# Expert queries in three goes instead of two, with tile 1's scores and tile 0's exponential between the second and the third

## The reference

```python
def peer_ffn(h, lp):
    q = (x @ lp['peer_wq']).reshape(t, PEER_HEADS, 2, PEER_HALF)          # 8 heads, 2 x 64
    sc = jnp.einsum('thpd,hpnd->thpn', q, lp['peer_subkeys'])             # 128 keys each
    sv, si = lax.top_k(sc, PEER_TOPK)                                     # 16
    cand = (sv[:, :, 0, :, None] + sv[:, :, 1, None, :]).reshape(t, PEER_HEADS, 256)
    top_v, top_p = lax.top_k(cand, PEER_TOPK)
    experts = jnp.take_along_axis(cidx, top_p, axis=-1)
    gates = jax.nn.softmax(top_v, axis=-1)
    # per token: sum over its 128 experts of gate * gelu(x . u[e]) * v[e]
```

## Time and profile before

| | us |
|---|---|
| median of 3 runs | 4885.16 |
| lowest and highest | 4881.96, 4885.67 |
| the profiled execution | 4879.89 |
| its span on the core | 4877.8 |

### The profile page before, as it was taken

How to read it: one execution, slowest core, us unless ns; L and a number is a source line. 1 busy time by engine, 2 the same in 40 slices (tenths; PEclk the granted TensorE clock), 3 DMA queues, 4 the chain that set the end, 5 groups by cost and what they waited for, 6 DMA issues and landing times.

```text
span 4877.8 us, 65715 instructions
## 1 busy us (share of the span) xinstructions
PE 4086.6 (84%) x23446; PEld 3534.7 (72%) x23446; DVE 3535.7 (72%) x6335; ACT 1394.0 (29%) x1987; POOL 1808.1 (37%) x1075
## 2 busy tenths in 40 slices
PE   6889999724499999999878999996336999999996
PEld 5866888423389888998767678883225898889885
DVE  2417224699989999999942272256998999999998
ACT  3236111212233332333232361112113333323331
POOL 1100000000088777877622000000001787778774
PEclk9989999868799999999978999997778999999998
DMA  5320112103499999999843101231134999999996
GB/s 211 121 84 1 52 69 98 71 21 94 126 395 401 390 394 369 402 397 396 329 182 137 58 1 61 78 113 39 46 101 167 405 406 384 393 375 401 393 397 253
DMA packets 326859, 1074.69 MB, mean 220 GB/s; under 512 B 25505, under 2 KB 123857, under 8 KB 275985
## 3 DMA queue, kind: packets, MB, share of 16 engines
q0 software_dynamic: 151168, 552.73, 29.2%
q1 hardware_dynamic: 75536, 464.03, 24.1%
q10 hardware_dynamic: 99968, 55.58, 3.8%
HBM read 1012.72 MB, written 59.51 MB: 220 GB/s over the span
## 4 chain that ended last, share of the span: by engine, by line
PE 35%; DVE 34%; DVEq 9%; POOL 8%; issue 8%; DMA 4%; ACT 2%; ACTq 0%; SPq 0%
PE PS L578 9%; PE PS L587 6%; PE PS L588 6%; PE PS L589 6%; DVE acc L1858 6%; DVE ring_lo L1828 5%; POOL got_a L553 4%; POOL got_b L553 4%; DVE ohB L1809 3%; DVEq L1850 3%; DVE spare L1858 2%; DMA ring<-weights 2%; DVEq L1835 2%; PE PS L582 2%; PE PS L750 2%
## 5 line engine op out<-in xcount | busy, mean ns | idle before, releaser
L553 POOL DMA_INDIRECT got_a<-u_rows,sidx x256 | 452.2, 1766 | 1331.0 <-DMA gate_matrix<-stg 1235.7
L1284 ACT CAST ring_hi<-ring 128x2048 fp32r<-128x2048 f32 x256 | 489.7, 1914 | 1265.7 <-DMA ring<-weights 1265.7
L587 PE MATMUL PS<-hT_hi,ring_hi 128*128 128x384 f32 x2048 | 687.4, 336 | 11.8 <-DVE ring_lo L1828 11.8
L589 PE MATMUL PS<-hT_hi,ring_lo 128*128 128x384 f32 x2048 | 687.0, 335 | 0.0
L588 PE MATMUL PS<-hT_lo,ring_hi 128*128 128x384 f32 x2048 | 686.2, 335 | 0.0
L587 PE MATMUL PS<-ring_hi,W_hi 128*128 128x512 f32 x1536 | 609.0, 396 | 54.5 <-DVE W_lo L1844 54.5
L588 PE MATMUL PS<-ring_lo,W_hi 128*128 128x512 f32 x1536 | 606.1, 395 | 0.0
L589 PE MATMUL PS<-ring_hi,W_lo 128*128 128x512 f32 x1536 | 605.7, 394 | 0.0
L1828 DVE TENSOR_TENSOR ring_lo<-ring,ring_hi 128x2048 fp32r<-128x2048 f32 x256 | 585.1, 2286 | 0.0
L553 POOL DMA_INDIRECT got_b<-v_rows,sidx x256 | 423.8, 1655 | 158.3 <-DVE acc L1858 90.3
L553 POOL DMA_INDIRECT got_b<-u_rows,sidx x256 | 422.1, 1649 | 139.8 <-issue 70.4
(11 more groups left out here) (278 smaller groups left out, 8551.7 us busy)
## 6 DMA issues: line engine op xcount, KB each, us to landing
ring<-weights SPq DMA_DIRECT2D x392, 1024.0 KB, 7.7
G<-gate_matrix SPq DMA_DIRECT2D x128, 384.0 KB, 8.5
gate_matrix<-stg ACTq DMA_DIRECT2D x10, 4096.0 KB, 15.9
gate_matrix<-stg ACTq DMA_DIRECT2D x2, 3584.0 KB, 17.3
x_wait<-x POOLq DMA_DIRECT2D x2, 2560.0 KB, 23.5
x<-x_wait ACTq DMA_DIRECT2D x10, 512.0 KB, 11.4
lnr<-lnrows POOLq DMA_DIRECT2D x4, 1024.0 KB, 5.0
got_a<-u_rows,sidx POOLq DMA_INDIRECT x256, 8.8
```

The source lines that it names most:

```text
L553: pool.indirect_dma_start(out=got[n % GB], out_offset=None, in_=u_rows[:, :] if phase % 2 == 0 else v_rows[:, :], in_offset=bass.IndirectO ...
L587: mm(out, a_hi, b_hi, start=first, stop=False)
L589: return mm(out, a_lo, b_hi, start=False, stop=final)
L1284: nc.scalar.copy(ring_hi[s][:, :], ring[:, s, :]).then_inc(hi_ready, 1)
```

## The change

The second go over the queries is cut in two. It now takes tile 1 alone (128 columns a matmul, two groups to a bank, as the first go), and a third go takes tiles 2 to 4 (384 columns a matmul). The third go reads the four blocks of `peer_wq` once more, so the weight stream has four more entries per layer (WQC), and the three slots are handed round in a new order. On PE, `score_tile(1)` moves from behind the turned token tiles to between the second and the third go. On ACT, `pick_tile(0)` (copy of tile 1's queries, wait for tile 0's best values, exponential, copy of tile 1's scores) moves from behind all query copies to the same place, with a drain ahead of it. Code on VectorE and GpSimd is unchanged; on SP only the order and number of loads change.

```diff
-MERGE, OUT, SUB, WQA, WQB, PEER = 37, 55, 59, 60, 64, 68
+MERGE, OUT, SUB, WQA, WQB, WQC, PEER = 37, 55, 59, 60, 64, 68, 72
-N_Q = 12
+N_Q = 16
-        last_use += [(q_full, N_Q, k + 1) for k in range(4)]
-        last_use += [(q_full, N_Q, 4 + 2 * (k + 1)) for k in range(4)]
+        last_use += [(q_full, N_Q, k + 1) for k in range(8)]
+        last_use += [(q_full, N_Q, 8 + 2 * (k + 1)) for k in range(4)]
...
                 for k in range(4):
                     wait_slot(pe, l, WQB + k)
                     w = ring[:, POSITION[WQB + k], :].rearrange("p (c n) -> p c n", c=KC)
+                    query(4 + k, (0, P), w, slice(P, 2 * P))
+                score_tile(1)
+                for k in range(4):
+                    wait_slot(pe, l, WQC + k)
+                    w = ring[:, POSITION[WQC + k], :].rearrange("p (c n) -> p c n", c=KC)
                     for hh in range(2):
-                        query(4 + 2 * k + hh, (hh * P,), w, slice(P, T))
+                        query(8 + 2 * k + hh, (hh * P,), w, slice(2 * P, T))
...
-                for t in range(1, NS + 1):
+                for t in range(2, NS + 1):
                     score_tile(t)
...
-                for j in range(4, N_Q):
+                for j in range(4, 8):
                     act.wait_ge(q_full, layer_at(l, N_Q, j + 1))
-                    nc.scalar.copy(qT2[:, j - 4, P:T], bank(4 + j % 4)).then_inc(q_ready, 1)
+                    nc.scalar.copy(qT2[:, 2 * (j - 4):2 * (j - 4) + 2, P:2 * P],
+                                   bank(4 + j % 4, 0, 256).rearrange("p (h n) -> p h n", h=2)).then_inc(q_ready, 1)
+                act.drain()
+                pick_tile(0)
+                for j in range(8, N_Q):
+                    act.wait_ge(q_full, layer_at(l, N_Q, j + 1))
+                    nc.scalar.copy(qT2[:, j - 8, 2 * P:T], bank(4 + j % 4, 0, TD)).then_inc(q_ready, 1)
...
                 act.drain()
-                for t in range(NS):
+                for t in range(1, NS):
                     pick_tile(t)
...
-            s[WQA + k] = s[WQB + k] = columns(peer_wq[l], 256 * k)
+            s[WQA + k] = s[WQB + k] = s[WQC + k] = columns(peer_wq[l], 256 * k)
```

## The result

| | before | after |
|---|---|---|
| median, us | 4885.41 (4 runs, 4881.96 to 4893.09) | 4819.52 (4 runs, 4815.98 to 4824.17) |
| the profiled execution | 4879.89 | 4820.70 |
| its span | 4877.8 | 4818.6 |

The ratio is 0.9862, 95% interval 0.9848 to 0.9876: 65.9 us less by the medians. The forecast was 4818.

The account below looks back on a forecast made before the run. VectorE's wait between tiles 0 and 1, behind the query matmuls, was taken as the bound. Removing 33.36 + 33.51 = 66.9 us from the median 4885.2 gave 4818 us, range 4810 to 4832.

Parts of the forecast that it names:

- The bound: VectorE between tiles 0 and 1: waiting for exponential and scores, 35.30 and 35.45 us from last reduction to MAX8.
- What is left of the gap: VectorE from tile 0's last reduction to tile 1's MAX8: 1.94 us remain per layer, so 66.9 us go.
- Second go, scores, exponential: PE and ScalarE, tile 1: go 17.3 us, scores 3.79; exponential 13.8 and score copy 11.6 us ahead of need.
- The third go: PE, queries of tiles 2 to 4: 43.5 us taken, 51.8 us at the other column price.
- The cover: Tile 2's scores stand 5.9 us before VectorE wants them; each us of lateness beyond costs 1 us per layer.
- The turning point: A third go 39.3 us late would gain nothing.
- The cut's own cost: PE's query matmuls: 2.8 us more per layer, beside VectorE's work.
- Loads: SP's queue: four more 1 MB weight loads per layer, each landing in 4.8 us, in time for PE.
- The rule against the trace: PE's clock: idle time between goes may repeat the ramp, moving the slack from 5.9 to about 5 us.
- Rival 1: Third go's cover fails in part, by column price and late fourth load: 8.9 us per layer, 4836 us; chance 0.10.
- Rival 2: The wait moves whole, or the gain is given back in the expert stretch: 4885 us; chance 0.04.
- Rival 3: PE's clock stays at half speed after the cut, making tile 2's scores late: 4905 us; chance 0.03.

Follow-up runs that it names:

- two runs with one half moved: Kernel before with only tile 0's exponential moved up: 4883.98 us; changed kernel with only that exponential put back behind the third go: 4887.08 us.
- all three delays: Changed kernel with the third go's first group computed 2, 4 or 8 more times: 4821.55, 4845.87 and 4881.60 us.
- the last experiment: Changed kernel with tile 0's exponential ahead of the copy of tile 1's queries on ScalarE: 4816.75 us, ratio 0.9867.
- the first three experiments: Kernel before with tile 0's exponential moved, 4883.98 us; changed kernel with it put back, 4887.08; changed kernel with it and tile 1's scores put back, 4887.23.
- the cut elsewhere: Changed kernel with the second go taking tiles 1 and 2 and the third tiles 3 and 4: 4819.04 us, ratio 0.9867.
- two more groups: Changed kernel with the third go's first group computed two more times, 10.3 us more PE work per layer: 4821.55 us, ratio 0.9877.
- eight more groups: Changed kernel with the third go's first group computed eight more times, 41.3 us more PE work per layer: 4881.60 us, ratio 0.9999.

## Why the prediction was right

**The bound.** Right. VectorE's gap between tiles 0 and 1 was the price, taken as the whole of 35.30 and 35.45 us from reduction to MAX8, not as the wait that was named. The two runs with one half moved show that this is the way to count it: counted by names, the halves would be worth 62.7 and 5 us, and they are worth 0 and 0.

**What is left of the gap.** Predicted 1.94 us per layer, measured 1.68 and 1.70. The 0.38 us of "issue" at the hand-over from tile 1 to 2 doesn't occur here. The gain was 33.6 + 33.75 = 67.4 us against 66.9.

**Second go, scores, exponential.** The go took 17.40 us against 17.3. Tile 1's scores were predicted to stand 24.6 us after the go's start (917.6 against 893.0) and stood after 23.0 (919.53 against 896.57). Tile 0's best values were there at 913.91, 1.6 us before ScalarE came for them, the lead that was predicted. The term that was off is the score tile: 2.06 us at the full clock, not 3.79. PE's idle time was foreseen (1.6 us, measured 1.58), but its score matmuls were priced by a row that follows a longer idle time.

**The third go.** Predicted 43.5 us between bounds of 43.5 and 51.8, measured 41.55, outside both. Both bounds were whole goes with a cold start in them (their first microseconds at a granted clock of 0.50), and this go has none, since the clock never fell. A group took 5.16 us (4.68 + 0.48 in ScalarE's rows), which is 6.87 x 3/4: the warm price per column is that of the old go. The row for it stood in the earlier trace rows and would have given 41.2 us. So an unseen shape was bounded by averages that hold a start-up cost, where the steady rate and the start should have been priced apart.

**The cover.** Predicted 5.9 us, measured 9.2 in the trace and by all three delays in the first layer. The 3.3 us are the 1.7 of the scores and the 1.9 of the third go, less 0.3 in small terms of the tail and the hand-over. Since both were on the safe side, the sum didn't change. The turning point moves from 39.3 to 9.2 + 33.7 = 42.9 us of lateness, and 41.3 us of added work came out at 0.9999.

**The cut's own cost.** Predicted 2.8 us of PE per layer from whole-go prices; back to back it is 0.6 to 0.9 us, for the same reason, and in the changed kernel all of it is covered. Loads: PE waited for none. Six issues between 895 and 940 us land after a median of 5.2 us, against 4.8 before:

```profile
ring<-weights SPq DMA_DIRECT2D x6, 1024.0 KB, 5.2
```

**The rule against the trace.** In the changed kernel the ramp didn't return in tile 1's scores and the third go. The second go pays it after 4.93 us of idle time, as the old second go did after 5.00. The prediction took the section HAM oscillation of the page TensorE: Matmul & The Clock Gate (the Trainium skill) to speak against the cut; but in that section's example PE waits for longer than it works between its bursts, and here it was idle for 1.58 us after 17.40 us of work. The trace shows no loss there. In the last experiment, with 3.06 us of idle time, the clock did fall and the next burst began cold, which is what the section describes, though there too PE had worked longer (17.30 us) than it idled. The prediction took the ramp to be possible and priced it at about 1 us of the cover; the run with the longer gap shows 1.1 us on the third go, and a further 1.7 us on the scores.

**The rivals.** Rival 1 was more pessimistic than needed in both of its terms. Rival 2 falls: over both layers the expert stretches of the four kernels that wait (before and the first three experiments) have a mean of 1119.65 us, and those of the four in which VectorE waits for at most 1.5 us (after, the cut elsewhere, two more groups, the clock) 1119.68, and the time between picks and the first gather is shorter by the full 34 us in both layers. Rival 3 needs a clock that stays low through the cut; the clock was at 1.00 through the third go. Its mechanism, a third go too late for tile 2, is real, as the delays show.

**Profiled time and median.** The sum was made against 4879.89 and carried to the median by a shift of 5.3 us, 4818.3. The median of after is 4819.52. The pair of profiled executions alone would have said 59.2 us; the difference lies in stretches that the change doesn't touch, each of which differs by no more than single executions do.

## What to carry to other kernels

When an engine waits for two things that come a few us apart, the profile gives the whole wait to the first and a small rest to the second. Price the gap from the last useful operation to the next one, and ask which of the inputs has to move; here moving one of them alone was worth nothing. Work cut in two to let one part out early needs only to be in time, and its cost doesn't count as long as the remaining part keeps its own cover: state that cover in us, and price an unseen shape by steady rate and start separately.

## What the runs showed of the hardware that I had not expected

Whether a short idle time of PE costs the clock isn't told by its length alone. The same 32 score records took 2.06 us at a granted clock of 1.00 in all 12 places in these traces where they follow 1.58 to 1.80 us of idle time. They follow 2.90 to 4.84 us in 48 places: in 45 of them they took 3.41 to 3.79 us, at about half the clock, and in three they took 2.06 to 2.48, at 0.79 to 1.00 (tile 2's scores in the second layer with eight more groups and in both layers of the last run). What decides in those three no run here isolates. The prediction had priced tile 1's scores at 3.79.

float32 matmuls of 128, 256, 384 and 512 columns cost nearly the same per column at the full clock: 41.55 us for 24,576 columns is 1.69 ns, 27.89 us for 16,384 is 1.70, and 6.87 us for 4,096 is 1.68; a group of the second go (8 x 2 matmuls of 128 columns) takes 3.57 us (3.20 + 0.37), 1.74 ns. So the smallest shape costs 4% more here, not the 19% that the averages of whole goes had suggested.
